# Order of VectorE's work at the ends of the FFNs, the starts of the mixers and the modulation bias in a two-block fp32 kernel

## What is computed

```python
for l in range(2):
    h = h + 0.5 * swiglu(rmsnorm(h), w_gate, w_up, w_down)        # FFN, 1024 -> 2816 -> 1024
    proj = rmsnorm(h) @ w_in[l]                                   # mixer, 28 tiles of 128 columns
    h = h + concat(retention(proj), diff_attention(proj)) @ w_out[l]
    h = h + 0.5 * swiglu(rmsnorm(h), ...)                         # second FFN
h = rmsnorm(h)[:, 16:]
...
mod = silu(c) @ w_mod + b_mod                                     # second block
x = second block(x, ctx, mod, ...)                                # ends in 32 experts, top 2
```

## Time and profile before

| | us |
|---|---|
| median of 3 runs (1801.21 to 1801.52) | 1801.39 |
| the profiled execution, its own time | 1802.41 |
| its span, first to last instruction | 1800.5 |
| TensorE products, busy | 1752.2 (97%) |
| VectorE, busy | 895.3 (50%) |
| ScalarE, busy | 696.2 (39%) |
| GpSimd, busy | 148.6 (8%) |
| mean granted TensorE clock | 0.993 |

### The profile page before, as it was taken

The page is one execution under the profiler, slowest core; times in us unless marked ns, Lnnn a source line. Parts: engine busy times, 40 slices in busy tenths (PEclk is TensorE's granted clock), DMA queues, the critical chain, the costliest instruction groups (busy, mean ns, idle before and its releaser), DMA issues.

```text
span 1800.5 us, 30540 instructions
## 1 busy us (share of the span) xinstructions
PE 1752.2 (97%) x12531; PEld 1428.6 (79%) x12532; DVE 895.3 (50%) x1560; ACT 696.2 (39%) x1169; POOL 148.6 (8%) x156
## 2 busy tenths in 40 slices
PE   8999999999999999999999999999889999999997
PEld 8999988899999999998899999577664444445442
DVE  6655666586655765576677665375321111121111
ACT  6444544364445543445455444543421111121110
POOL 1000132210000000022312000001200000000000
PEclk9999999999999999999999999999989999999998
DMA  9555465454554554556545554321379999999996
GB/s 382 197 171 167 161 234 188 164 179 173 172 178 159 181 177 164 176 190 219 211 178 205 175 178 164 85 80 47 152 309 402 422 422 422 422 422 422 422 422 264
DMA packets 89177, 425.81 MB, mean 237 GB/s; under 512 B 17504, under 2 KB 34144, under 8 KB 42976
## 3 DMA queue, kind: packets, MB, share of 16 engines
q1 hardware_dynamic: 88624, 421.01, 62.2%
q10 hardware_dynamic: 432, 3.10, 0.4%
HBM read 423.03 MB, written 1.05 MB: 236 GB/s over the span
## 4 chain that ended last, share of the span: by engine, by line
PE 84%; SPq 5%; DMA 3%; ACT 3%; DVE 3%; issue 1%; DVEq 0%; POOL 0%; POOLq 0%; ACTq 0%
PE ps L657 18%; PE ps L659 17%; PE ps L658 17%; PE ps L1270 9%; SPq L591 5%; PE ps L1313 4%; PE ps L1251 2%; PE ps L982 2%; PE ps L994 2%; PE ps L1227 2%; DMA con<-stream_expert 2%; DMA ring<-stream_expert 2%; PE ps L751 1%; PE ps L988 1%; ACT w_split L1367 1%
## 5 line engine op out<-in xcount | busy, mean ns | idle before, releaser
L1778 DVE TENSOR_TENSOR w_split<-ring,w_split 128x1024 fp32r<-128x1024 f32 x335 | 422.3, 1267 | 353.7 <-ACT w_split L1367 352.8
L657 PE MATMUL ps<-x_hi,w_split 128*128 128x272 f32 (+1 forms) x1856 | 541.8, 292 | 5.3 <-DVE arena L1937 1.8
L659 PE MATMUL ps<-x_hi,w_split 128*128 128x272 f32 (+1 forms) x1856 | 534.6, 288 | 0.0
L658 PE MATMUL ps<-x_lo,w_split 128*128 128x272 f32 (+1 forms) x1856 | 532.5, 287 | 0.0
L1367 ACT ACTIVATE w_split<-ring 128x1024 fp32r<-128x1024 f32 x335 | 350.7, 1054 | 361.6 <-PE ps L659 360.4
L657 PEld LDWEIGHTS ps<-x_hi,w_split 128*128 128x128 f32 x1856 | 350.1, 189 | 18.3 <-issue 9.6
L658 PEld LDWEIGHTS ps<-x_lo,w_split 128*128 128x128 f32 x1856 | 350.2, 189 | 0.3
L659 PEld LDWEIGHTS ps<-x_hi,w_split 128*128 128x128 f32 x1856 | 350.0, 189 | 0.0
L657 PE MATMUL ps<-hid_hi,w_split 128*128 128x272 f32 (+1 forms) x704 | 202.1, 287 | 3.8 <-DVE arena L1879 3.8
L659 PE MATMUL ps<-hid_hi,w_split 128*128 128x272 f32 (+1 forms) x704 | 201.8, 287 | 0.0
L658 PE MATMUL ps<-hid_lo,w_split 128*128 128x272 f32 (+1 forms) x704 | 201.4, 286 | 0.0
(11 more groups left out here) (407 smaller groups left out, 2188.9 us busy)
## 6 DMA issues: line engine op xcount, KB each, us to landing
ring<-stream_expert SPq DMA_DIRECT2D x132, 1024.0 KB, 22.8
ring<-stream_ffn SPq DMA_DIRECT2D x131, 1024.0 KB, 4.8
arena<-stream_expert SPq DMA_DIRECT2D x40, 1024.0 KB, 23.7
ring<-stream_in SPq DMA_DIRECT2D x27, 1024.0 KB, 4.9
ring<-stream_mod SPq DMA_DIRECT2D x24, 1024.0 KB, 7.0
con<-stream_expert SPq DMA_DIRECT2D x20, 1024.0 KB, 23.2
ring<-stream_out SPq DMA_DIRECT2D x12, 1024.0 KB, 4.9
ring<-stream_in SPq DMA_DIRECT2D x42, 256.0 KB, 3.8
```

The costliest lines, as they stand in the source:

```text
L657: pe.matmul(to, w[:, 0, k], hi, start=first, stop=False)
L658: pe.matmul(to, w[:, 0, k], lo, start=False, stop=False)
L659: return pe.matmul(to, w[:, 1, k], hi, start=False, stop=last_)
L1778: nc.vector.tensor_tensor(w[:, 1], half_of(n), w[:, 0].bitcast(fp32), ALU.subtract).then_inc(split_ready, 1)
```

## The change

Three places in VectorE's program change their order. In the last pair of every FFN (j = 21) only the first of two weight halves is done before the evictions of the gate and the up tile; the second follows them. In step 5 of every mixer the evictions of tiles 0 and 1 come before the weight half instead of behind it. The bias of the modulation is added at the end of step 25 (`MOD_TURN_AT`) instead of in step 26. No other engine's program changes, and no instruction is added or removed.

```diff
--- before.py
+++ after.py
@@ -1871,12 +1871,14 @@
 
                 for j in range(F):
                     if j >= 2:
-                        weights_lo(n0 + 2 * j + 6)
+                        weights_lo(n0 + 2 * j + (6 if j < F - 1 else 5))
                     bank = 2 * (j % 4)
                     dve.wait_ge(split_used, n0 + 2 * j + 1)
                     nc.vector.tensor_tensor(gate_act[:, j % 4, t:T], ps[:, bank, 0:T - t], rstd[:, t:T], ALU.mult).then_inc(gate_ready, 1)
                     dve.wait_ge(split_used, n0 + 2 * j + 2)
                     nc.vector.tensor_tensor(hid[:, j, t:T], ps[:, bank + 1, 0:T - t], rstd[:, t:T], ALU.mult).then_inc(gate_up_used, 1)
+                    if j == F - 1:
+                        weights_lo(n0 + 2 * j + 6)
                     dve.drain()
                     dve.wait_ge(gate_act_ready, f * F + j + 1)
                     nc.vector.tensor_tensor(hid[:, j, t:T], hid[:, j, t:T], gate_act[:, j % 4, t:T], ALU.mult).then_inc(hid_ready, 1)
@@ -2047,7 +2049,8 @@
                                             ALU.subtract).then_inc(y_split_ready, 1)
 
                 for x in range(5, len(TILES)):
-                    weights_lo(n0 + x + 5)
+                    if x > 5:
+                        weights_lo(n0 + x + 5)
                     if x == 23:
                         factors(1, slice(4, 13))
                     if 0 <= x - 10 < 8:
@@ -2056,6 +2059,8 @@
                         greatest(8)
                     for tile in EVICT_AT[x]:
                         evict(tile)
+                    if x == 5:
+                        weights_lo(n0 + x + 5)
                     if 0 <= x - 11 < units:
                         combine(x - 11)
                     if x in RET_SCORES:
@@ -2071,8 +2076,9 @@
                         ret_stats(0, 4).then_inc(stat_ready, 1)
                     if x in (22, 23, 24, 25):
                         diff_head_lo(x - 22)
+                    if x == MOD_TURN_AT:
+                        mod_bias(l)
                     if x == 26:
-                        mod_bias(l)
                         if l == 0:
                             diff_lo(4, y_lo[:, 4:8, 0:META], ps[:, 5, 0:P].rearrange("p (h q) -> p h q", h=HEADS)[:, :, 0:META], y_hi[:, 4:8, 0:META])
                         last_centre()
```

## The result

The changed kernel takes **1787.93 us** (median of four runs, 1786.76 to 1788.88) against 1801.38 (four runs, 1801.21 to 1801.52): a ratio of 0.9924 with an interval of 0.9911 to 0.9936; by the medians the gain is 13.5 us, by the interval 11.5 to 16.0. Five more runs of it, in another group, gave 1787.07 to 1790.31; all nine have a mean of 1788.1. The kernel before, run beside every experiment, has a mean of 1801.36 over 54 runs (1799.9 to 1803.7), so the gain by the means is 13.2 us. Disturbed executions, the longest of 6099 us, are left out of all numbers here. The forecast was 11.4 us and 1790.0. The measured time stands at the very edge of the range (1787.8 to 1794.4): the median is 0.1 us inside its low end, and 0.9924 times 1801.39, which is 1787.7, is 0.1 us outside.

What follows compares the result with a forecast made beforehand. TensorE, 97% busy, was taken as the bound, the last quarter running through DMA. FFN ends 4.8, mixer starts 2.3 and modulation bias 4.3 sum to 11.4 us, from 1801.39 to 1790.0 us; range 1787.8 to 1794.4.

Steps and rivals of the forecast that it cites:

- The bound and the places: TensorE bounds the kernel, busy 97% of the span; seven waits for VectorE at the edited places, 8.8 us of standstill.
- FFN ends: Ends of the four FFNs: evictions ahead of the second weight half remove four TensorE waits, 4.8 us.
- Mixer starts: Start of both mixers: evicting tiles 0 and 1 first removes a whole TensorE wait, 1.15 us twice, 2.3 us.
- Modulation bias: Layer 0, steps 26 and 27: earlier bias saves 3.28 us of waiting and 1.23 of half clock, less 0.2; 4.3 us.
- The low part: Layer 0, step 27: TensorE needs the low part of the first rows (L2028) from VectorE, giving back 0.2 us.
- Passing through the expert stream: Last quarter, DMA-bound: expert transfers wait for work that moves with TensorE, so the whole gain reaches the end.
- rival 1: Part of the wait time stays: no clock drop before, tight handovers in step 27 or mixer starts; 1792.8 us, chance 0.14.
- Rivals 3, 4 and 5: Expert stream hides gain, 1801.4 (0.04); another releaser, at most 4.8 us less (0.03); less clock, slower, 1813 (0.03).
- rival 2: Clock falls elsewhere, behind second-block waits: 1.4 us per stretch, two give 1787.2 or 1792.8 us; chance 0.06.

Runs made afterwards that it cites:

- before_busy_wait: Kernel before, with 21 unread TensorE products added ahead of its wait for the modulation bias in layer 0; two times, 1799.71 and 1801.22 us.
- before_busy_wait2: Same program run again under another name: kernel before with 21 unread products in the wait for the bias; mean 1799.77 us, ratio 0.9992.
- after_again: The changed kernel run once more, unchanged; five runs, median 1788.46 us, ratio 0.9926.
- after_delay8: The changed kernel with 24 more unused products (2.8 us) in the last FFN; six runs, mean 1794.8 us.
- only_ffn_ends: The kernel before with only the change at the FFN ends; six runs, mean 1795.37 us, ratio 0.9968.
- only_mixer_starts: The kernel before with only the change in step 5 of the mixers; nine runs, mean 1798.56 us, ratio 0.9984.

## Why the prediction was wrong, step by step

- **The bound and the places** were right. TensorE was waiting for VectorE at these seven places, and all three entries of the earlier trace rows vanished.
- **FFN ends**: 4.91 us for 4.8. Lost start-to-start time and the slower first product are what a wait costs; its idle time alone (3.8) would have been 1.1 too little.
- **Mixer starts**: 2.27 us for 2.3. The new wait of 0.18 us in layer 1 is the size that the Trainium skill's rule (SBUF — State Buffer, Who interferes with whom) allowed for, though not at tile 9. I had taken 0. The timeline after, in the second mixer:

```profile
807.37 0.77 POOL L2529 TENSOR_TENSOR arena<-arena 128x272 f32<-128x272 f32 x1
807.82 1.40 DVE L1778 TENSOR_TENSOR w_split<-ring,w_split 128x1024 fp32r<-128x1024 f32 x1 [1.43 <-ACT w_split L1367]
...
810.85 0.73 PE L799 MATMUL ps<-arena 64*128 64x272 f32 x4 [0.17 <-ACT arena L1478]
```

  The subtraction takes 1.40 us for 1.23: it runs beside GpSimd for 0.32 us, until 808.14, and loses 0.17; in before it took 1.23 and GpSimd was done 0.07 us after it began. VectorE's reduction, ScalarE's L1478 and TensorE's L799 behind it are late by the same 0.17. Layer 0 has no such wait.
- **Modulation bias**: 4.36 us for 4.3, made of 3.24 for the wait (forecast 3.28) and 1.17 for the half clock from turn to turn (1.23), less 0.05 behind it. The low part did hold the turn, by about 0.1 us for the 0.2 taken off; that 0.1 is already in the 1.17. before_busy_wait and before_busy_wait2 bear out the split into waiting and half clock.
- **Passing through the expert stream**: right. The first expert transfer is issued at 1273.56 us in after_again and 1287.59 in before, and the lead at 1342 us (13.65) is the lead at 1669; 0.1 us of it is gone at the last product (13.56).
- **Slots, queues, tight handovers (rival 1)**: none but the 0.18 us. **Rivals 3, 4 and 5** fell with the lines above.
- **The step that failed is the clock, rival 2.** I priced half clock at the one place where before's profile had it behind an edited wait and asked of the rest only whether it might go "elsewhere", at 0.06 and in equal parts up and down. Yet before's own profile had a low stretch behind the wait of 2.1 us and another around the ranks, and the prediction names and weighs neither. At a wait that already has its low stretch a shift can only take it away, so the odds there were not even. Its loss in both profiles of the changed kernel gives 1.6 us, and 11.5 + 1.6 = 13.1 us, where 13.2 was measured by the means. For the profiled executions this is shown; for the timed ones the mean clocks agree with it, and the interval of the gain (11.5 to 16.0 us) begins just at what the edits give. Rival 2's own figure was 1787.2, for two stretches missed.
- **The range** was too narrow on that side by the same step: rival 2's own low figure lay outside it. It took the time of before as known to 0.3 us from three runs, and the executions of one kernel differ by 2 us and more.

The Trainium skill says (TensorE: Matmul & The Clock Gate, Part 1, What's actually happening) that TensorE's activity is judged over stretches that run on regardless of the kernel. The runs agree: the grid of the low stretches lay differently in two executions of one program, and one wait of unchanged length did and didn't bring the half clock. But I used the rule only to take 1.2 us off a gain, and it says as much about stretches that a shift removes.

**Open**: which timed runs had the half clock behind the wait of 2.1 us. The gap of 1.13 us is open too. It has a part in after_delay8, which pays 6.7 us for 2.8 of work. Against the first profile of the changed kernel its profile is 7.2 us late: 2.8 for the work, 1.6 for the half clock behind the wait of 2.1 us, 2.7 in the last product group (the gap of 1.13 and products that take 10.84 us for 9.23) and 0.1 elsewhere.

## What to carry to other kernels

When an engine's order is changed, cost a wait by the start-to-start time lost and the slow restart, and check that every moved piece of work fits ahead of the next need; that gave 11.4 us for 11.5 here. Then list every stretch of low clock in the whole profile, also in stages that the edit does not touch: each can be worth a microsecond or more, and a shift can drop or call it, as can the next execution of the same kernel. Where TensorE must stand still for some microseconds, products that nothing reads can be cheaper than rest; measure the whole kernel with them, since one set of them lost more in the last product group than it had gained.

## What the runs showed of the hardware

- A wait of 3.2 us went with no half clock (only_ffn_ends), with the stretch of the earlier trace rows or with one twice as long (only_mixer_starts). One of 2.11 us brought 1.56 us of loss or nothing, in eight and five profiles, also in two profiles of one program; it did where a point of the low stretches' grid came 0.4 to 1.3 us behind the wait's end, and did not at 2.4 to 2.9 us.
- 21 extra products in a wait made a kernel no slower and by its mean 1.6 us faster.
- A VectorE subtraction of 1.23 us took 1.40 to 1.79 us beside GpSimd, and two of them 3.04 us, while GpSimd's operations went from 0.77 to as much as 1.76 us.
- A product group without any recorded wait inside it was broken for 1.13 us when 20 or 24 products were added much earlier, for 0.55 us or not at all with 21, and never with 12.
